# Expert weights in units of up to 1024 inner columns: longer rows per transfer, two banks for gate and for up, pairs without an end of their own

## What is computed

```python
def _swiglu(h, wg, wu, wd):
    return (jax.nn.silu(h @ wg) * (h @ wu)) @ wd

def _moe(h, router, wg, wu, wd):
    logits = (h @ router).astype(jnp.float32)
    top_v, top_i = lax.top_k(logits, TOP_K)               # TOP_K = 2
    w = jax.nn.softmax(top_v, axis=-1)
    combine = jnp.sum(jax.nn.one_hot(top_i, N_EXPERTS, dtype=jnp.float32) * w[..., None], axis=-2)
    out = jnp.zeros_like(h)
    for e in range(N_EXPERTS):                            # 8 experts
        out = out + combine[..., e:e + 1].astype(h.dtype) * _swiglu(h, wg[e], wu[e], wd[e])
    return out
# wg, wu: (8, 1024, 3584)   wd: (8, 3584, 1024)   all float32: 352 MB
```

## Time and profile before

| | us |
|---|---|
| median of 3 runs | 1908.9 |
| the runs | 1905.53, 1908.9, 1914.71 |
| span of the profiled execution | 1913.1 |
| the experts, first gather to last scatter product, in it | about 887 to 1902 |

### The profile page before, as it was taken

The page is one execution under the profiler, slowest core; times in us unless marked ns, Lnnn a source line. Parts: engine busy times, 40 slices in busy tenths (PEclk is TensorE's granted clock), DMA queues, the critical chain, the costliest instruction groups (busy, mean ns, idle before and its releaser), DMA issues.

```text
span 1913.1 us, 23772 instructions
## 1 busy us (share of the span) xinstructions
PE 1819.7 (95%) x8964; PEld 1480.6 (77%) x8964; DVE 1335.5 (70%) x1280; ACT 1050.9 (55%) x1009; POOL 116.7 (6%) x126
## 2 busy tenths in 40 slices
PE   4999989999999999987999999999999999999997
PEld 2986578888888888566888878887788888888875
DVE  2578556333333376746888889888889898889886
ACT  3333734222122153545677777776777777777764
POOL 1120800000000012400000000000000000000000
PEclk8999989999999999998999999999999999999999
DMA  8325823522432224735999999999999999999994
GB/s 292 126 88 208 321 67 79 140 95 83 110 88 94 72 89 132 273 124 177 354 348 368 355 333 363 362 348 344 360 334 376 342 350 378 327 359 355 367 348 158
DMA packets 245912, 472.85 MB, mean 247 GB/s; under 512 B 10547, under 2 KB 60565, under 8 KB 245805
## 3 DMA queue, kind: packets, MB, share of 16 engines
q1 hardware_dynamic: 241712, 468.14, 69.3%
q10 hardware_dynamic: 4092, 3.20, 0.6%
HBM read 470.26 MB, written 1.05 MB: 246 GB/s over the span
## 4 chain that ended last, share of the span: by engine, by line
PE 52%; DMA 20%; DVE 16%; ACT 7%; issue 4%; POOL 0%; SPq 0%; DVEq 0%; ACTq 0%; POOLq 0%
PE bank L543 14%; PE bank L545 14%; PE bank L544 14%; DVE parts L1707 8%; DMA raw<-in_moe_w_gate_dram 7%; DMA raw<-in_moe_w_down_dram 6%; ACT parts L1409 5%; DMA raw<-in_moe_w_up_dram 5%; DMA raw<-in_ada_w_dram 2%; PE bank L561 2%; PE bank L1047 1%; DVE parts L1692 1%; PE bank L790 1%; PE bank L779 1%; PE bank L771 1%
## 5 line engine op out<-in xcount | busy, mean ns | idle before, releaser
L1707 DVE TENSOR_TENSOR parts<-raw,parts 128x2048 fp32r<-128x2048 f32 x336 | 765.3, 2289 | 113.0 <-ACT parts L1409 111.6
L1409 ACT ACTIVATE parts<-raw 128x2048 fp32r<-128x2048 f32 x336 | 642.7, 1919 | 260.1 <-DMA raw<-in_moe_w_up_dram 104.7
L543 PE MATMUL bank<-parts,XEr 128*128 128x512 f32 x896 | 356.1, 397 | 8.4 <-DVE parts L1707 6.1
L545 PE MATMUL bank<-parts,XEr 128*128 128x512 f32 x896 | 349.8, 390 | 0.0
L544 PE MATMUL bank<-parts,XEr 128*128 128x512 f32 x896 | 349.1, 390 | 0.0
L1270 ACT ACTIVATE parts<-raw 128x2048 fp32r<-128x2048 f32 (+1 forms) x62 | 113.2, 1831 | 270.0 <-PE bank L545 249.9
L1692 DVE TENSOR_TENSOR parts<-raw,parts 128x2048 fp32r<-128x2048 f32 (+1 forms) x62 | 135.8, 2194 | 136.4 <-ACT parts L1270 136.1
L543 PEld LDWEIGHTS bank<-parts,XEr 128*128 128x128 f32 x896 | 168.3, 188 | 47.9 <-DVE parts L1707 8.3
L545 PEld LDWEIGHTS bank<-parts,XEr 128*128 128x128 f32 x896 | 168.2, 188 | 36.2
L544 PEld LDWEIGHTS bank<-parts,XEr 128*128 128x128 f32 x896 | 168.6, 188 | 32.7
L543 PE MATMUL bank<-parts,HTr 128*128 128x512 f32 x448 | 176.1, 393 | 2.8 <-DVE HTr L1707 2.5
(11 more groups left out here) (245 smaller groups left out, 2279.3 us busy)
## 6 DMA issues: line engine op xcount, KB each, us to landing
raw<-in_moe_w_gate_dram SPq DMA_DIRECT2D x112, 1024.0 KB, 7.0
raw<-in_moe_w_up_dram SPq DMA_DIRECT2D x112, 1024.0 KB, 7.2
raw<-in_moe_w_down_dram SPq DMA_DIRECT2D x112, 1024.0 KB, 6.8
raw<-in_ada_w_dram SPq DMA_DIRECT2D x28, 1024.0 KB, 8.6
more<-in_ada_w_dram SPq DMA_DIRECT2D x20, 1024.0 KB, 7.5
raw<-in_w_in_dram SPq DMA_DIRECT2D x12, 1024.0 KB, 5.1
raw<-in_ffn_w_gate_dram SPq DMA_DIRECT2D x22, 512.0 KB, 4.0
raw<-in_ffn_w_up_dram SPq DMA_DIRECT2D x22, 512.0 KB, 5.3
```

The source lines that it names most:

```text
L543: nc.tensor.matmul(out, st[0], mv[0], start=start, stop=False)
L545: return nc.tensor.matmul(out, st[1], mv[0], start=False, stop=stop)
L1409: nc.scalar.activation(parts[:, n % PARTS, 0, :], raw[:, r, :], ACT.Copy).then_inc(hi_ready, 1)
L1707: return nc.vector.tensor_tensor(out, a, b, op)
```

## The change

An expert's 7 slices become 4 **units** of 2, 2, 2 and 1 slices (`UNIT_BLOCKS`). A pair is 8 units. The size of an item (1 MB), the number of items (84 for each pair), of matmuls and of transposes, and the two rings of four slots stay.

- A gate or up item of a 1024-column unit holds two 128-row blocks of 1024 columns (rows of 4 KB). The last unit of each expert keeps 512 columns. A down item gives each partition two adjacent rows (8 KB in one piece); the transposes read HE with a step of two elements to match.
- Item order in a unit: gate(u) x 2B, up(u) x 2B, down(u-1) x 2B', where B is the slices of this unit and B' those of the one before.
- PSUM: G and U get two banks each, Y two, and one pair R serves turns, gathers, scatters. `turn(u)` writes up to 8 transposes at once, so the silu, the product HE, and both parts of HTr are up to 1024 columns wide. SGE, HE and HTr have one buffer instead of two.
- PE's order in a unit: gate(u), turn(u-1), up(u), then for the third unit of an expert the gather of the next expert, for the second unit the first half of the previous expert's scatter, then down(u-1), then the scatter's second half.
- ACT and DVE have their extra work placed by item: each piece stands behind the split of the item that is four places after the one on which it depends (on DVE ahead of the split for HE, XF and ACC). HTr stands at the first up item of the unit.
- One semaphore (`expert_item`) counts multiplied items in place of six. The last down of a pair is done in the next iteration: pairs run on without an end of their own, and only the last one has its closing.

```diff
-PAIR_SLICES = 2 * EF_SLICES
-PAIR_ITEMS = 6 * PAIR_SLICES
+UNIT_BLOCKS = (2, 2, 2, 1)
+UNITS = len(UNIT_BLOCKS)
+PAIR_UNITS = 2 * UNITS
...
+                        rows = io["moe_w_down"][0][bass.ds(e, 1), r0:r0 + 2 * P, :].rearrange("e (p k) n -> p (e k) n", p=P)
...
+                        k = 4 // blocks
+                        r0 = j * k * P
+                        rows = io["moe_w_" + kind][0][bass.ds(e, 1), r0:r0 + k * P, c0:c0 + blocks * SLICE]\
+                            .rearrange("e (k p) n -> p (e k) n", p=P)
...
@@ PE @@
+                        gate_or_up(i, v, at, p0, "gate", G)
...
+                            if q == 2:
+                                pe.wait_ge(scatter_read, i * 8 + (4 * (e0 + u // UNITS) + 1))
+                            if q == 3:
+                                pe.wait_ge(xe_lo, i * 2 + (j0 + u // UNITS + 2))
+                                pe.wait_ge(xe_hi, i * 2 + (j0 + u // UNITS + 2))
+                            turn(i, u - 1)
+                        gate_or_up(i, v, at, p0, "up", U)
...
+                        if q == 2 or scattering:
+                            pe.wait_ge(ht_ready, i * PAIR_UNITS + (u0 + u))
+                        if q == 2:
+                            gather(i, u // UNITS + 1)
+                        if scattering:
+                            scatter(i, u // UNITS - 1, 0)
+                        if v or not opening:
+                            down(i, u - 1, v - 1, at)
+                        if scattering:
+                            scatter(i, u // UNITS - 1, 1)
...
+                def turn(i, u):
+                    pe.wait_ge(up_read, i * PAIR_UNITS + (u0 + u + 1))
+                    blocks = UNIT_BLOCKS[u % UNITS]
+                    hidden = HE[:, 0:blocks * SLICE].rearrange("p (half c j) -> p half j c", half=2 * blocks, j=2)
+                    for c in range(blocks):
+                        for m in range(4):
+                            mm = nc.tensor.transpose(R[c][:, m * P:(m + 1) * P], hidden[:, 2 * c + m // 2, m % 2, :], ident)
@@ ACT @@
+                    for m, (_, n) in enumerate(order):
+                        if m >= PARTS or not opening:
                             split_expert(i, n, part)
...
+                        (kind, v, j), done = order[m - PARTS]
+                        u, q = p0 * PAIR_UNITS + v, v % UNITS
+                        if (kind, v, j) == last_item("gate", v):
+                            gate_silu(i, u, done)
+                        if kind == "up" and j == 0 and u:
+                            turned(i, u - 1)
```

More of the change, by code:

```diff
@@ L456, in build, with unit_items, places_of, last_item @@
             (ada_loaded if is_ada else split_loaded)[n] = loads_before[r]
[L459 to L473, removed]
+        def unit_items(opening):
+            out = []
+            for u in range(PAIR_UNITS):
+                n = 2 * UNIT_BLOCKS[u % UNITS]
+                out += [("gate", u, j) for j in range(n)] + [("up", u, j) for j in range(n)]
+                if u or not opening:
+                    out += [("down", u - 1, j) for j in range(2 * UNIT_BLOCKS[(u - 1) % UNITS])]
+            return out
+        opening_items, later_items = unit_items(True), unit_items(False)
+        opening_at = {item: n for n, item in enumerate(opening_items)}
+        later_at = {item: len(opening_items) + n for n, item in enumerate(later_items)}
+        closing_at = {("down", -1, j): PAIRS * PAIR_ITEMS - LAST_DOWN + j for j in range(LAST_DOWN)}
+        def places_of(opening):
+            return opening_at if opening else later_at
+        def last_item(kind, u):
+            return kind, u, 2 * UNIT_BLOCKS[u % UNITS] - 1
+        def multiplied(n, part):
+            return CREDIT + part * PAIRS * PAIR_ITEMS + n + 1
+        def slot_free(n, part):
+            return part * PAIRS * PAIR_ITEMS + n + 1
         v_bank, a_bank = [], []
@@ L1073, in turn_places @@
                         mm.then_inc(places_full, 1)
-                def pair(i, opening):
[L1077 to L1119, removed]
-                            pe.wait_ge(places_read, PAIRS * (part + 1))
[L1121 to L1127, removed]
-                            turn_places()
[L1129 to L1138, removed]
@@ new lines, in weights, with gate_or_up @@
+                def weights(i, n, rows):
+                    pe.wait_ge(lo_ready, i * PAIR_ITEMS + (BASE + part * PAIRS * PAIR_ITEMS + n + 1))
+                    return [parts[:, n % PARTS, s, :].rearrange("p (k n) -> p k n", k=rows) for s in range(2)]
+                def gate_or_up(i, v, at, p0, kind, b):
+                    q = v % UNITS
+                    blocks = UNIT_BLOCKS[q]
+                    rows = 4 // blocks
+                    e = p0 * 2 + v // UNITS
+                    for j in range(2 * blocks):
+                        hi, lo = weights(i, at[kind, v, j], rows)
+                        if q == 0 and kind == "gate" and (j * rows) % 4 == 0:
+                            pe.wait_ge(xe_ready, i * 4 + (2 * (j0 + e) + j * rows // 4 + 1))
+                        for kk in range(rows):
+                            k = j * rows + kk
+                            x = XEr[:, e % 2, :, k, :]
+                            for c in range(blocks):
+                                col = slice(c * SLICE, (c + 1) * SLICE)
+                                mm = three(b[c][:, :], (x[:, 0, :], x[:, 1, :]), (hi[:, kk, col], lo[:, kk, col]), k == 0, k == KT - 1)
+                        mm.then_inc(expert_item, 1)
@@ L2231, in experts @@
                     split_expert(0, n, part)
-                gathered(0, 0)
+                gathered_high(0, 0)
+                gathered_low(0, 0)
                 for n in range(2, PARTS):
```

294 lines of the change are left out of this document (161 added, 133 removed).

## The result

The changed kernel takes **1951.6 us** (median of 4 runs, 1949.6 to 1953.6), the kernel before 1911.2 us (median of 4: the three runs of the table above and 1913.4). The ratio is 1.0213, with a 95% interval of 1.019 to 1.0236: 40 us slower. The profiled execution has a span of 1947.8 us, 34.7 more than that of before.

What follows compares the result with a forecast made beforehand. PE was taken to bound the kernel, with transfers just fast enough. Pauses that go -12, new pause +28, clock +17 and opening and end +3 gave +36 us: 1945 us for the median, range 1920 to 1963.

Steps and rivals of the forecast that it cites:

- Its deciding step: In each expert's fourth unit, PE has only two up items between turn and down while HTr is 1024 wide, so it pauses.
- PE sets the pace: In the expert stage PE bounds the time; transfers are just fast enough and four item slots absorb their jitter.
- The new pause: PE waits for HTr before down in each expert's fourth unit: 3.5 us each, eight experts, +28 us (23 to 35).
- The clock: After each of the eight new pauses PE's granted clock falls to half: 2.1 us each, +17 us (14 to 20).
- The rival in which it holds: The eight fourth-unit pauses come but the granted clock stays up: +19 us, 1928 us, chance 0.19.
- Pauses that go: -12: PE's waits for low parts, HTr and issue, at pair ends and from late items, shrink: -12 us (7 to 14).
- Loop start: PE's 1.27 us pause at the start of each of three iterations was said to stay; no new one forecast.
- Opening and end: +3: PE waits for item 4 at the experts' opening, +1.4 us, and the last turn's hand-over lies bare, +1.5; together +3.
- Strided transposes: nothing: PE's transposes reading HE with a step of two cost nothing; bound from above 25 us.
- The rival of half pace: Strided transposes run at half pace, +25 us on top of the forecast; part of the worse case, chance 0.09.
- Transfers: Longer rows of items land at most 0.2 us earlier, or bring nothing by the 512 B figure; PE feels it only through pauses.

Runs made afterwards that it cites:

- HTr early: Changed kernel with ACT's copy of HTr and DVE's low part of it both moved one item earlier: 1924.2 us, ratio to the kernel before 1.006.
- HTr early on one engine alone: Changed kernel with only ACT's copy of HTr one item earlier: 1951.5 us; with only DVE's low part of HTr one item earlier: 1956.1 us.
- The filled pause: Changed kernel with three useless float32 matmuls of 512 columns on PE between each fourth unit's up and down products: 1931.5 us, ratio 1.0094.
- the run with early HTr and no step: Changed kernel with HTr one item earlier, PE's loop written out, places' transposes ahead, 4 KB down rows, transposes without step: 1917.7 us, ratio 1.002.
- all three pairs of runs: 8 KB against 4 KB down rows: kernel before (1917.5, 1911 us), HTr one item earlier with loop written out (1915.8, 1917.7), HTr ahead of that item (1908.2, 1910.4).
- repaired form: Changed kernel with PE's loop written out, places' transposes ahead, and HTr on ACT and DVE ahead of the item it stood behind: 1908.2 us, ratio 0.9987.
- the kernel before, written out: The kernel before with PE's hardware loop over pairs written out: 1908.9 us, ratio 0.9993.
- the loop written out: Changed kernel with the hardware loop over the later pairs written out on PE alone: 1941.3 us, ratio 1.0141.
- ACT's half of the early HTr: Changed kernel with only ACT's copy of HTr one item earlier, DVE's low part left in place: 1951.5 us, ratio 1.0212.

## Why the prediction was right, and where its terms were off

The forecast was 1945 us within 1920 to 1963, slower with 0.83; it is 1951.6. Its deciding step holds as it was written, and the runs bear it out.

- **PE sets the pace.** Right: the pauses and slow stretches given to PE came out as time, and where they were taken away the time fell.
- **The new pause.** Floor worked out as 2.75 us of idle, measured 2.81; largest worked out 4.25, measured 3.96. Eight of them, at the place named, 26 us for the 28 forecast. With HTr early the time fell by 27 us, with HTr early on one engine alone by nothing, which leaves the chain over both.
- **The clock.** Forecast 17, measured 11.2 at these pauses. I had it fall at all eight, at 2.1 each; it fell at six, at 1.9 on average (1.4 to 3.0). The filled pause shows that this is time on top of the pause. The rival in which it holds was wrong for most pauses and right for two. Of the five pauses of 2.8 us three brought the clock down and two did not, so my argument from the length alone did not hold.
- **Pauses that go: -12.** Mis-sized. The pauses of PE's weight loads between 900 and 1885 add up to 19.8 us before, and all but 0.4 went. The table of waits that I used starts at 960 and so left out 1.6 of them; I kept 3.8 us for a loop's start that was a pair's end, and took 12 of the 14 that were left.
- **Loop start: left out.** 6.1 us of new pauses without a releaser and 3.4 of slow clock behind them. I had written that the start "stays, since three iterations stay", and so looked for no new one. This is the term that the sum lacked.
- **Opening and end: +3.** 1.6 and 1.6 measured, both where they were put.
- **Strided transposes: nothing.** Measured 2 us on the kernel before. In the changed kernel the weight loads take 209 ns where they were 139, and a turn of eight 0.87 us where the run with early HTr and no step has 0.79, so 2.3 us in all. The statement of the Trainium skill (page "SBUF — State Buffer", section "Door 1: The DMA port swizzle") that two accesses to a 16-byte line keep full bandwidth does not hold for these loads. The rival of half pace was wrong too, at a tenth of its 25 us.
- **Transfers.** A landing of gate items went from 7.0 to 6.8 us, of up items from 7.2 to 6.8, of down items from 6.8 to 6.9. But PE was slower then, and with the pauses repaired gate items land in 7.0 again and up items in 7.2. By the 512 B for full rate of the Trainium skill (page "DMA: Bandwidth & Descriptors", section "Specifications") nothing was to be had from longer rows. No run here shows a time that contradicts it, but ACT's waits for down items are shorter with 8 KB rows in all three pairs of runs (57.0 for 59.8, 41.8 for 53.8, 65.3 for 83.1), so it isn't confirmed either. Rows of 4 KB for gate and up were never tried alone.

The sum with the measured terms: 26.0 + 11.2 + 9.5 + 3.2 + 2.3 - 19.4 = 32.8 us, beside 34.7 between the two spans. The medians lie 40.4 apart. Of the 5.7 between, 3.5 are in the kernel before, whose profiled run lies that much above its median, and 2.1 in the changed kernel, whose profiled run lies below its own.

The total came nearer than its terms, and that part is luck. Against the measured terms the new pause, the clock and the pauses that go were off by 15 us in one direction (too slow a kernel), the loop's start, the transposes and the end by 12 in the other. That the new pause and the clock carry the change is not luck: their place, number and floor were worked out ahead.

Where did the change's own gain go? Its repaired form has no pause at the ends of pairs, and no wait for HTr but the last, and still takes the time of the kernel before. Its traces show part of a gain. The span is 1905.1 us beside 1913.1, and the pauses of PE's weight loads between 900 and 1885 add up to 8.3 us beside 19.8; the strided transposes take back 2.3 of that. But the kernel before, written out, shows only 8.0 us of such pauses in a span of 1907.4, though its time is no different from that of the kernel before. So these pauses change from run to run, and the 19.8 that I counted on come from one slower than the median. There was less to win than I thought. The 4 us between the medians (1908.2 and 1912.0) lie within the noise.

The transfers look like the next bound, since ACT waits for them in the repaired form as it did before (gate items 91.6 us, up items 63.9). A window over its experts speaks against it:

```profile
920.00:1870.00 950.00, 948.60 (x4396) 789.17 (x4395) 839.76 (x489) 692.98 (x452) 0.00 (x0) 1.00 0.97 357
```

PE is busy 948.60 of 950 us, and its weight loads wait 3.9 us for low parts in the whole stage. PE still sets the pace there; what the transfers cost it is, by this trace, at most those few us. The DMA share of 0.97 says that there is little room behind that, but no run with less to transfer was made.

## What to carry to other kernels

When a stage is cut into larger units of which the last is smaller, check the small one by itself: the work that used to cover a hand-over shrinks with it, while the hand-over comes from the larger unit ahead and is at its longest. In an in-order queue, place a hand-over that the bound engine waits for ahead of the prefetch work, not behind it, and on both engines of its chain: moving one alone gained nothing, and made the other wait. Where an engine's pause can't be avoided, see what the clock does after it, since here a pause of 3 us cost up to 3.0 more.

## What the hardware showed that I had not expected

- Pauses of PE of the same shown length of 2.8 us sometimes brought the granted clock to half for 3.4 us (three of five in the changed kernel) and sometimes did not (none of five with the loop written out). All those of 3.1 us or more did, in both. The pause of 2.15 us ahead of the experts, which every version has, left the clock up in nine of the thirteen traces and brought it down in four (for instance at 895.2 with ACT's half of the early HTr). So the length of a pause alone does not tell.
- Filler work in the eight pauses kept the clock up, worth 11 us, without shortening the waits.
- PE's two jumps back in a loop were followed by pauses of 2.2 and 3.5 us in one program, and by none in a program with a few instructions more, nor in the kernel before.
- Transposes that read with a step of two float32 load their weights in 204 to 209 ns, not 139; on PE's pace that was 0.04 us for four.
